# A 256-token two-layer block: 64 tokens of the product-key expert layer gathered row by row for VectorE, the other 192 with u in native fp32

## The chip, the cores and the metric

One Trainium2 chip, one of its NeuronCores. The metric is the device time of one execution in microseconds (us). The kernel is a single program written engine by engine: TensorE (PE), VectorE (DVE), ScalarE (ACT), GpSimd (POOL) and SyncE (SP, which only issues DMAs), with every wait written out by hand.

## What is computed

The reference is two transformer-like layers over 256 tokens of width 1024. The change concerns the expert layer (PEER) at the end of the first. Each token has 8 heads; each head picks 16 of 16384 experts by product keys; `u` and `v` are 16384 x 1024 fp32 tables.

```python
q = (h @ w_q).reshape(B, S, 8, 2, 128)
sc = einsum('bshpd,phnd->bshpn', q, keys)
v1, i1 = top_k(sc[..., 0, :], 16); v2, i2 = top_k(sc[..., 1, :], 16)
best, pos = top_k((v1[..., :, None] + v2[..., None, :]).reshape(..., 256), 16)
idx = take_along_axis((i1[..., :, None] * 128 + i2[..., None, :]).reshape(..., 256), pos)
gates = softmax(best)
act = gelu(einsum('tkd,td->tk', u[idx], h))        # 128 picks a token
out = einsum('tk,tkd->td', gates * act, v[idx])
```

## The kernel before

**How the work is staged.** All weights, about 240 MB, stream through the chip once, in 512 KB units of 128 partitions x 1024 fp32 (the table `STREAMS`): 18 + 4 + 16 + 4 + 4 + 8 units of the first layer's mixers, 16 of `w_pq`, then 128 units of `u`, 128 of `v`, then the second layer. SP fetches unit i into `raw[i % 4]` once unit i-4 has been used up.

**How a unit is multiplied.** TensorE's fp32r product keeps fewer bits than fp32, so every operand is split in two: ACT rounds the unit into `whi` (helper `act`, line 1154), DVE or POOL subtracts to get `wlo` (helper `tt`, line 1712, or POOL's line 2555), three slots each (`NSPL = 3`), and PE does three products (line 433):

```python
def three(o, a, b, start, stop):
    mm(o, a[0], b[0], start, False)
    mm(o, a[0], b[1], False, False)
    return mm(o, a[1], b[0], False, stop)
```

**The dense expert layer.** Rather than gather, the kernel computes all experts for all 256 tokens. Stage u (`lin_T`, 128 units): unit n holds 128 experts; 8 stationary tiles of 128 x 128 against `hTh`/`hTl` (normed tokens, transposed), 256 columns, 24 matmuls a unit; ACT applies the gelu to two units at a time from a PSUM bank into `acts`. Stage v (128 units): unit n's 128 experts are the contraction; `acts[:, n, :]` is split into two halves (`cut_acts`, one ACT and one DVE instruction of 256 columns) and is the stationary operand, `down(b, m, h)` for two token blocks b and two halves h of the width, 12 matmuls of 512 columns a unit, added up in banks 0 to 3 over all 128 units.

**Routing and gates.** What is not picked must be weighted with zero. `routing(b)` on DVE finds, for the tokens of block b, the picks and gates (MAX, MATCH_REPLACE, MAX_INDEX and compares); PE transposes them (line 442, three transposes a block); DVE copies them to `iT`, `row_b`, `col_b`, `gate2`. `gates(half)` builds, for 8 tokens at a time, one-hot matrices on DVE (`build`: `oh`, `og_eq`, `og`), multiplies them on PE (16 small matmuls) and multiplies `acts` by the result on DVE (`weigh`): 32 groups a half, 64 in all.

**What sets the order.** Side work is written as generators in a `Side` list; each engine calls `side.step()` once behind each unit, so that the same step of each engine's generator stands beside the same unit. `routing(0)`, `routing(1)` run in the first 62 units of u (`U1_STEPS` gives the number of steps behind each unit), then `side.drain()`; `gates(0)` in the last 66 units of u, `gates(1)` in the first 62 of v. POOL makes `wlo` for the first 62 units of u (`on_pool`), DVE for the others. DVE's loop over v runs two units ahead:

```python
for n in range(128):
    lo(BASE["v"] + n + 2)
    if n == 62:
        side.drain()
    cut_acts(n + 2)
    side.step()
```

SP's queue has the constants of the second layer (`con2`, 1345 KB) and `gf`, `w2c`, `mem` between units of v. `bridge()` adds the banks into `xres` behind stage v and normalises.

## Time and profile before

| | |
|---|---|
| median of 3 runs | 1445.1 us (1443.62 to 1445.19) |
| profiled execution, first to last instruction (span) | 1441.8 us |
| between the span and the median of the runs | 3.3 us |
| DMA moved | 245 MB |
| stage u, units 1 to 62, from the trace's clock | 266.0 to 444.8 us |
| stage u, units 63 to 128 | 444.8 to 654.3 us |
| stage v | 654.3 to 1034.0 us |

The page gives the profiled execution its span; no other time of its own is given for it, so the span stands for it. All times inside are on the span's clock. A busy PE means that some matmul was in flight; how fast they follow one another is read from start to start, since their durations overlap.

### The profile page before, as it was taken

The numbers are of one execution on the slowest core, as the hardware profiler recorded it, in microseconds if no ns is written. First come the engines' busy times: TensorE is split into PE (matmuls) and PEld (weight loads), VectorE is DVE, ScalarE is ACT, GpSimd is POOL, SyncE is SP. The second block draws the span as 40 slices with busy tenths as digits, with TensorE's granted clock in tenths as the row PEclk, the third lists the DMA queues.
The fourth block names the chain that finished last, engine by engine and source line by source line (L and its number), as shares of the span: only waits on it lengthen the run. The fifth ranks groups of instructions, "written<-read, shape, count | busy, mean of one in ns | idle before, by whom it ended". The sixth has DMA issues, their size and how long they took to land.

```text
span 1441.8 us, 25221 instructions
## 1 busy us (share of the span) xinstructions
PE 1422.6 (99%) x10281; PEld 1290.2 (89%) x10281; DVE 967.4 (67%) x1752; ACT 738.5 (51%) x1066; POOL 212.7 (15%) x122
## 2 busy tenths in 40 slices
PE   8999999999999999999999999999999999999997
PEld 7989989999999999998777778888899788899986
DVE  5565674693944777778888876655577864677754
ACT  5674654545454444444444445544567754655543
POOL 5000000488883000000000000000114100000000
PEclk9999999999999999999999999999999999999999
DMA  6433456455555545445545466555543453455552
GB/s 241 142 132 125 138 157 216 141 186 180 187 180 182 170 162 174 164 164 173 174 164 174 164 222 245 181 185 188 175 147 118 159 177 112 154 188 185 181 190 103
DMA packets 67219, 245.07 MB, mean 170 GB/s; under 512 B 7456, under 2 KB 7712, under 8 KB 66848
## 3 DMA queue, kind: packets, MB, share of 16 engines
q1 hardware_dynamic: 66960, 243.19, 50.5%
q8 instruction: 82, 1.34, 0.4%
q14 instruction: 33, 0.27, 0.1%
q10 hardware_dynamic: 144, 0.26, 0.0%
HBM read 242.37 MB, written 1.05 MB: 169 GB/s over the span
## 4 chain that ended last, share of the span: by engine, by line
PE 77%; issue 14%; DVE 4%; ACT 4%; POOL 1%; DMA 0%; POOLq 0%; SPq 0%; DVEq 0%; ACTq 0%
PE bank L433 76%; ACT A L1154 2%; DVE wlo L1712 1%; ACT whi L1154 1%; PE bank L442 1%; DVE A L1712 1%; ACT L1154 1%; DVE A L1708 0%; DVE xres L1712 0%; DMA xres<-in_x 0%; POOL wlo L2555 0%; ACT hTh L1154 0%; DVE small L2361 0%; DVE small L1712 0%; POOL small L2561 0%
## 5 line engine op out<-in xcount | busy, mean ns | idle before, releaser
L1712 DVE TENSOR_TENSOR wlo<-raw,whi 128x1024 fp32r<-128x1024 f32 (+1 forms) x375 | 458.1, 1223 | 334.3 <-ACT whi L1154 333.9
L1154 ACT ACTIVATE whi<-raw 128x1024 fp32r<-128x1024 f32 (+1 forms) x450 | 472.9, 1053 | 401.3 <-PE bank L433 401.3
L433 PE MATMUL bank<-hTh,whi 128*128 128x256 f32 x1944 | 555.5, 286 | 2.0 <-DVE wlo L1712 1.3
L433 PE MATMUL bank<-hTl,whi 128*128 128x256 f32 x1944 | 548.6, 282 | 0.0
L433 PE MATMUL bank<-hTh,wlo 128*128 128x256 f32 x1944 | 548.0, 282 | 0.0
L433 PEld LDWEIGHTS bank<-hTh,whi 128*128 128x128 f32 x1944 | 367.0, 189 | 5.9 <-DVE wlo L1712 2.1
L433 PEld LDWEIGHTS bank<-hTh,wlo 128*128 128x128 f32 x1944 | 366.0, 188 | 0.0
L433 PEld LDWEIGHTS bank<-hTl,whi 128*128 128x128 f32 x1944 | 365.5, 188 | 0.3 <-issue 0.2
L433 PE MATMUL bank<-whi,hTh 128*128 128x512 f32 (+2 forms) x552 | 218.4, 396 | 0.2
L433 PE MATMUL bank<-wlo,hTh 128*128 128x512 f32 (+2 forms) x552 | 215.0, 390 | 0.0
L433 PE MATMUL bank<-whi,hTl 128*128 128x512 f32 (+2 forms) x552 | 214.9, 389 | 0.0
L2555 POOL TENSOR_TENSOR wlo<-raw,whi 128x1024 fp32r<-128x1024 f32 x73 | 175.2, 2401 | 267.6 <-ACT whi L1154 263.7
L1154 ACT ACTIVATE A<-bank 128x512 f32<-128x512 f32 (+2 forms) x163 | 90.7, 563 | 225.9 <-PE bank L433 216.2
L2561 POOL TENSOR_TENSOR small<-small 128x1 f32<-128x1 f32 x16 | 9.5, 593 | 935.9 <-DVE small L1709 932.1
L433 PEld LDWEIGHTS bank<-whi,hTl 128*128 128x128 f32 x552 | 104.0, 188 | 23.8
L433 PEld LDWEIGHTS bank<-whi,hTh 128*128 128x128 f32 x552 | 104.1, 189 | 23.4 <-DVE wlo L1712 0.8
L433 PEld LDWEIGHTS bank<-wlo,hTh 128*128 128x128 f32 x552 | 104.2, 189 | 22.2
L433 PE MATMUL bank<-A 128*128 128x128 f32 (+9 forms) x472 | 69.9, 305 | 0.0
L433 PEld LDWEIGHTS bank<-A 128*128 128x128 f32 (+4 forms) x472 | 59.5, 183 | 6.5 <-issue 2.5
L1712 DVE TENSOR_TENSOR hTl<-A,hTh 128x256 fp32r<-128x256 f32 x126 | 52.6, 418 | 0.5 <-ACT hTh L1154 0.5
L1154 ACT ACTIVATE hTh<-A 128x256 fp32r<-128x256 f32 x126 | 50.6, 401 | 1.9 <-DVE A L1715 1.9
L1715 DVE SCALAR_TENSOR_TENSOR A<-bank,A 128x512 f32<-128x512 f32 (+1 forms) x76 | 49.4, 658 | 2.3 <-PE bank L433 2.2
(178 smaller groups left out, 1391.8 us busy)
## 6 DMA issues: line engine op xcount, KB each, us to landing
raw<-in_u SPq DMA_DIRECT2D x128, 512.0 KB, 3.3
raw<-in_v SPq DMA_DIRECT2D x128, 512.0 KB, 3.3
raw<-in_w_up SPq DMA_DIRECT2D x44, 512.0 KB, 3.3
raw<-in_w_down SPq DMA_DIRECT2D x22, 512.0 KB, 3.2
raw<-in_w_in_t SPq DMA_DIRECT2D x17, 512.0 KB, 3.4
raw<-in_w_in_g SPq DMA_DIRECT2D x16, 512.0 KB, 3.3
raw<-in_w_out SPq DMA_DIRECT2D x16, 512.0 KB, 4.0
raw<-in_w_pq SPq DMA_DIRECT2D x16, 512.0 KB, 3.5
```

The lines of the kernel that those rows point to most:

```text
L433: return e.matmul(o, l, r, start=st, stop=sp_, skip_group_check=True)
L442: return e.transpose(o, i, ident[0:k, 0:k])
L1154: return e.activation(o, i, func, **kw)
L1712: return e.tensor_tensor(o, a, b, op)
L1715: return e.scalar_tensor_tensor(o, a, z, b, op0, op1, **kw)
L2555: e.tensor_tensor(l, raw[i % NRAW][:, :], h.bitcast(F32), ALU.subtract).then_inc(s["lo_pool"], 1)
L2561: e.tensor_tensor(st[:, 2:3], st[:, 3:4], mhalf, ALU.pow).then_inc(s["n_rstd"], 1)
```

## The change

The tokens are divided: tokens 64 to 255 (`TD` = 192) stay in the dense computation; tokens 0 to 63 (`TG` = 64) leave it.

- **Stage u** (`lin_u`): PE multiplies `raw` itself by `h_full` (the tokens in fp32, one DVE add before the stage) in native fp32: 8 matmuls of 192 columns a unit. No `whi`, no `wlo` for u, on any engine; `raw[i % 4]` is free when PE is done with it.
- **Stage v**: `mixed_block` (4 matmuls a unit) has a stationary operand of which 64 columns are the low halves of tokens 64 to 127 and 64 the high halves; the two parts of its result are in the partitions 0 to 63 and 64 to 127 of banks 0 and 1 and are added at the end (`v_low`, `fold`). `dense_block` (6 matmuls) is the old product for tokens 128 to 255. 10 matmuls of 512 columns a unit. `cut_acts`: 192 columns, two ACT instructions and one DVE.
- **Gates**: 24 groups a half; `gates(1)` begins 16 steps later.
- **The 64 tokens**: 64 x 128 picks are 8192 rows of u and as many of v, 4 KB each. Two tokens' halves share the partitions (64 picks in partitions 0 to 63, the other 64 picks of the same tokens in 64 to 127), so one indirect DMA of POOL's fetches 128 rows, 512 KB, into one of 6 buffers `got`. 64 such gathers of `u_rows`, 64 of v, 67 MB in all. DVE takes each (`take`): for u one multiply with `h_rows` that also sums along the row (a dot product a partition), for v one multiply-add into `v_sum`. `due(n)` says how many takes are done by unit n: none before unit 26, then one every second unit, one a unit for units 62 to 127, and one every second unit of v until 86. ACT makes the gelu of 16 dots at a time at units 78, 94, 110 and 126 (`COEF_AT`). `fold_rows` sums the two halves on PE at unit 118 of v.
- **Moved**: `U1_STEPS` goes from 66 steps in 62 units to (1, 1, 1, 2); SP's four constant loads stand at other units of v; the second layer's memory norm 20 units later; `routing` storage and other tiles at other addresses.

```diff
+def is_u(i):
+    return BASE["u"] <= i < BASE["v"]
+def hi_count(i):
+    return i + 1 - min(max(i + 1 - BASE["u"], 0), 128)
...
-    if BASE["u"] <= slot < BASE["u"] + 62:
-        return True
...
+        if is_u(i):
+            out.append(("w", i + 1))
+            continue
...
-U1_STEPS = (1,) * 13 + (2,)
+U1_STEPS = (1, 1, 1, 2)
...
+def due(n):
+    if n < 26:
+        return 0
+    if n < 62:
+        return (n - 24) // 2
+    if n < 128:
+        return 19 + n - 62
+    return 85 + (n - 128) // 2
+COEF_AT = (78, 94, 110, 126)
...
+            def lin_u(n0, n1, steps=(1,)):
+                for n in range(n0, n1):
+                    i = BASE["u"] + n
+                    bk = 4 + pair[0] % 3
+                    if n % 2 == 0:
+                        use(bk)
+                    e.wait_ge(s_raw[i % NRAW], 16 * (i // NRAW + 1))
+                    wv = t3(raw[i % NRAW][:, :], KD)
+                    for k in range(KD):
+                        ins = mm(banks[bk][:, n % 2 * 256:n % 2 * 256 + TD], wv[:, k, :], hTf[:, k, TG:T], k == 0, k == KD - 1)
+                    ins.then_inc(s["w"], 1)
...
+                def mixed_block(m, h):
+                    w = wv[m - both[0]]
+                    for part in range(2):
+                        ins = mm(banks[h][:, :], cut(m, BOTH_M), w[part][:, h * 512:(h + 1) * 512], m == 0 and part == 0,
+                                 m == 127 and part == 1)
+                    return ins
+                def dense_block(m, h):
+                    w = wv[m - both[0]]
+                    return three(banks[2 + h][:, :], [cut(m, z) for z in (HI_D, LO_D)],
+                                 [z[:, h * 512:(h + 1) * 512] for z in w], m == 0, m == 127)
...
+                    e.wait_ge(s["fold_in"], 2)
+                    for h in range(2):
+                        ins = mm(banks[h][TG:P, :], ident[0:TG, 0:TG], v_low[0:TG, h * 512:(h + 1) * 512], False, True)
+                    ins.then_inc(s["fold"], 1)
...
+                if n == 118:
+                    e.wait_ge(s["x_done"], 2 * PICKS)
+                    e.wait_ge(s["eye"], 1)
+                    for h in range(2):
+                        use(6 + h)
+                        ins = mm(banks[6 + h][0:TG, :], fold_rows, v_sum[:, h * 512:(h + 1) * 512])
...
+                if b == 0:
+                    e.wait_ge(s["rt_dve"], 2)
+                    for q, dst in enumerate((tab, tab_up)):
+                        z = slice(q * PICKS, q * PICKS + PICKS)
+                        stt(dst[0:TG, 0:PICKS].bitcast(U32), sel_i[1][0:TG, z], float(P), sel_i[0][0:TG, z], ALU.mult, ALU.add)
+                        e.tensor_copy(dst[0:TG, PICKS:2 * PICKS], bex[0:TG, z]).then_inc(s["x_tab"], 1)
...
+            def take(x):
+                g = x % PICKS
+                z = got[x % NBUF]
+                e.wait_ge(s_got[x % NBUF], 16 * (x // NBUF + 1))
+                if x < PICKS:
+                    if x == 0:
+                        e.wait_ge(s_dup, 16)
+                    stt(z, z, 1.0, h_rows, ALU.mult, ALU.mult, accum_out=dots[:, g:g + 1]).then_inc(s["x_done"], 1)
+                    return
...
+                    e.wait_ge(s["x_done"], x)
+                    stt(v_sum, z, coef[:, g:g + 1], v_sum, ALU.mult, ALU.add).then_inc(s["x_done"], 1)
...
+            tt(hTf[:, :, TG:T], hTv[0][:, :, TG:T].bitcast(F32), hTv[1][:, :, TG:T].bitcast(F32), ALU.add).then_inc(s["h_full"], 1)
             side.lists[0] += [routing(0), routing(1)]
-            lin_T(BASE["u"], 62, steps=U1_STEPS)
+            lin_T(BASE["u"], 62, None, take_due, steps=U1_STEPS)
             side.drain()
             side.lists[0] += [gates(0), gates(1)]
-            lin_T(BASE["u"] + 62, 66)
+            lin_T(BASE["u"] + 62, 66, None, lambda u: take_due(u + 62))
...
+                take_due(n + 128)
                 side.step()
...
+            e.wait_ge(s["h_rows"], 1)
+            e.dma_start(h_rows[TG:P, :], h_rows[0:TG, :]).then_inc(s_dup, 16)
+            e.wait_ge(s["x_tab"], 2)
+            e.dma_start(tab[TG:P, :], tab_up[0:TG, :]).then_inc(s_tab, 16)
+            e.wait_ge(s_tab, 16)
+            e.wait_ge(s["sc_pe"], 8)
+            v_rows = wdram["v"].rearrange("n p d -> (n p) d")
+            for x in range(2 * PICKS):
+                g = x % PICKS
+                if x >= NBUF:
+                    e.wait_ge(s["x_done"], x - NBUF + 1)
+                e.indirect_dma_start(got[x % NBUF], None, u_rows if x < PICKS else v_rows,
+                                     bass.IndirectOffsetOnAxis(ap=tab[:, g:g + 1].bitcast(U32), axis=0)
+                                     ).then_inc(s_got[x % NBUF], 16)
+                if x == 2 * PICKS - 1:
+                    rstd(2)
```

**Where instructions stand now.** Three places carry the prediction. The first is PE's order at the second block's transposes in the first 62 units of u (`keep` holds the identity, `A` the picks). Before, they stand behind unit 56 of u:

```order
L433 MATMUL bank<-hTh,whi 128x256
L433 MATMUL bank<-hTl,whi 128x256
L433 MATMUL bank<-hTh,wlo 128x256
L442 MATMUL bank<-keep,A 128x128 [waits s_sc_act,s_rt_dve]
L442 MATMUL bank<-keep,A 128x128 x2
L433 MATMUL bank<-hTh,whi 128x256 [waits s_ev_act,s_lo_pool]
```

Of the change (behind unit 48 of u; the first block's stand behind unit 24):

```order
L494 MATMUL bank<-h_full,raw 128x192 [waits s_raw1]
L494 MATMUL bank<-h_full,raw 128x192 x7
L503 MATMUL bank<-keep,A 128x128 [waits s_sc_act,s_rt_dve]
L503 MATMUL bank<-keep,A 128x128 x2
L494 MATMUL bank<-h_full,raw 128x192 [waits s_raw2,s_ev_act]
```

A unit is 8 matmuls that wait for the DMA alone, and the same transposes with the same wait on DVE (`s_rt_dve`) come 8 units of u earlier.

The second is DVE's order where `routing(1)` nears the gates of block 1 (`picks` holds dots and coefficients, `G` the gathered rows). Of the change:

```order
L1828 TENSOR_TENSOR A<-bank,A 128x512 x3
L1831 SCALAR_TENSOR_TENSOR G,picks<-G 128x1024 [waits s_got2]
L2152 TENSOR_REDUCE A<-A 128x128 [waits s_own_dve]
L1828 TENSOR_TENSOR bank<-A,bank 128x512 [waits s_own_dve]
L1828 TENSOR_TENSOR bank<-A,bank 128x512 x3
L1828 TENSOR_TENSOR A<-bank,A 128x512 [waits s_own_dve]
L1828 TENSOR_TENSOR A<-bank,A 128x512 x3
L1831 SCALAR_TENSOR_TENSOR G,picks<-G 128x1024 [waits s_got3]
L2152 TENSOR_REDUCE A<-A 128x128 [waits s_own_dve]
L2155 TENSOR_REDUCE A<-A 128x8 [waits s_rt_act]
L2157 RECIPROCAL A<-A 128x8 [waits s_own_dve]
L1828 TENSOR_TENSOR A<-A 128x128 [waits s_own_dve]
```

The takes are new rows inside the routing; ten of them stand between the first block's `iT` copy and the last row shown, whose end the second transposes wait for.

The third is DVE's order in the first 47 units of v. Of the change, two units:

```order
L1828 TENSOR_TENSOR wlo<-raw,whi 128x1024 [waits s_hi]
L1828 TENSOR_TENSOR hT<-A,hT 128x192 [waits s_ca_hi]
L1828 TENSOR_TENSOR wlo<-raw,whi 128x1024 [waits s_hi]
L1828 TENSOR_TENSOR hT<-A,hT 128x192 [waits s_ca_hi]
L1831 SCALAR_TENSOR_TENSOR G<-G,picks 128x1024 [waits s_x_done,s_got2]
L1831 SCALAR_TENSOR_TENSOR A<-bank,A 128x64x8 [waits s_g_pe,s_ev_act]
L1828 TENSOR_TENSOR oh<-iota_b,row_b 128x1024 [waits s_g_pe]
L1828 TENSOR_TENSOR og_eq<-iota_b,col_b 128x512 [waits s_g_og]
L1828 TENSOR_TENSOR og<-og_eq,gate 128x1024 [waits s_own_dve]
```

Before, the same eight rows without the take, and with 256 in place of 192.

## Rows read from the trace of the kernel before

**Rows 1.** The page, part 1: busy us of each engine (share of the span), instructions

```profile
PE 1422.6 (99%) x10281; PEld 1290.2 (89%) x10281; DVE 967.4 (67%) x1752; ACT 738.5 (51%) x1066; POOL 212.7 (15%) x122
```

**Rows 2.** Stretches (first us:last us length, busy per engine (instructions), PEclk, DMA share, GB/s)

```profile
266.00:444.80 178.80, 178.80 (x1493) 178.80 (x1493) 119.36 (x452) 87.63 (x100) 147.52 (x62) 1.00 0.54 178
...
654.30:1034.00 379.70, 379.59 (x2048) 303.19 (x2049) 270.50 (x397) 178.91 (x271) 1.10 (x2) 1.00 0.56 188
```

**Rows 3.** Timeline of PE (start us, length us): fp32r products of 512 columns, two gate groups

```profile
701.32 0.40 PE L433 MATMUL bank<-whi,hTh 128*128 128x512 f32 x1
701.55 0.40 PE L433 MATMUL bank<-wlo,hTh 128*128 128x512 f32 x1
...
451.01 0.66 PE L433 MATMUL bank<-og,oh 128*128 128x64 f16 x16
...
647.27 0.66 PE L433 MATMUL bank<-og,oh 128*128 128x64 f16 x16
```

**Rows 4.** Timeline of PE: runs of fp32 products of 128 and of 256 columns

```profile
258.89 7.31 PE L433 MATMUL bank<-A 128*128 128x128 f32 x64
...
1202.88 3.62 PE L433 MATMUL bank<-A 128*128 128x256 f32 x16
```

**Rows 5.** Groups by shape, whole span: durations of those products and of a load (mean ns)

```profile
L433 PE MATMUL bank<-A 128*128 128x256 f32 x80 | 18.6, 378 | 0.0
L433 PE MATMUL bank<-A 128*128 128x128 f32 x136 | 16.2, 275 | 0.0
...
L433 PEld LDWEIGHTS bank<-A 128*128 128x128 f32 x312 | 42.3, 191 | 3.4 <-issue 1.2 <-DVE A L1712 0.2
```

**Rows 6.** Timeline of DVE in the routing (in brackets the idle time before, and who ended it)

```profile
347.21 0.56 DVE L2048 COPY iT<-bank 128x384 f32<-128x384 f32 x1 [19.19 <-PE bank L442]
...
408.56 0.41 DVE L1712 TENSOR_TENSOR A<-A 128x128 f32<-128x128 f32 x1
428.17 0.56 DVE L2048 COPY iT<-bank 128x384 f32<-128x384 f32 x1 [19.20 <-PE bank L442]
```

**Rows 7.** The nearest rows to a take: a product of this shape, and a sum read

```profile
L1715 DVE SCALAR_TENSOR_TENSOR A<-A 128x1024 f32<-128x1024 f32 x1 | 1.3, 1277 | 0.0
...
209.19 0.08 DVE L1715 DVE_READ_ACCUMULATOR A<-xres 128x1 f32 x1
209.31 0.22 DVE L1709 TENSOR_SCALAR small<-small 128x1 f32<-128x1 f32 x1
```

**Rows 8.** Timeline of DVE at the first gate groups (stage u, with wlo on DVE)

```profile
447.03 1.23 DVE L1712 TENSOR_TENSOR wlo<-raw,whi 128x1024 fp32r<-128x1024 f32 x1 [15.03 <-ACT whi L1154]
448.17 0.68 DVE L1712 TENSOR_TENSOR oh<-iota_b,row_b 128x1024 f16<-128x1024 f16 x1
...
449.83 1.22 DVE L1712 TENSOR_TENSOR wlo<-raw,whi 128x1024 fp32r<-128x1024 f32 x1
```

**Rows 9.** Groups of DVE by shape, 660 to 840 us (busy us, mean ns, idle before)

```profile
L1712 DVE TENSOR_TENSOR wlo<-raw,whi 128x1024 fp32r<-128x1024 f32 x59 | 72.0, 1221 | 26.1 <-ACT whi L1154 26.1
L1712 DVE TENSOR_TENSOR hTl<-A,hTh 128x256 fp32r<-128x256 f32 x59 | 24.6, 418 | 0.0
L1715 DVE SCALAR_TENSOR_TENSOR A<-bank,A 128x512 f32<-128x512 f32 x29 | 19.8, 682 | 0.0
```

**Rows 10.** A 20 us stretch of stage v with gates, and the densest DMA of the trace

```profile
700.00:720.00 20.00, 20.00 (x128) 15.88 (x127) 17.17 (x28) 8.74 (x13) 0.00 (x0) 1.00 0.51 165
...
8.00:16.00 8.00, 6.95 (x57) 6.38 (x55) 7.09 (x22) 6.18 (x15) 7.09 (x7) 1.00 0.99 377
```

**Rows 11.** DMA issues: KB each, median us from issue to landing

```profile
raw<-in_u SPq DMA_DIRECT2D x128, 512.0 KB, 3.3
A<-in_gf SPq DMA_DIRECT2D x2, 512.0 KB, 4.6
```

**Rows 12.** Timeline: DVE beside a POOL instruction of two SBUF inputs

```profile
1045.40 2.79 POOL L2623 TENSOR_TENSOR A<-A 128x128 f32<-128x128 f32 x4
1045.93 1.47 DVE L1712 TENSOR_TENSOR wlo<-raw,whi 128x1024 fp32r<-128x1024 f32 x1
```

More of the change, by code:

```diff
@@ L33 @@
 GATE_UP = 2.0 ** 15
+TG = 64
+TD = T - TG
+NG = TD // OB
+NBUF = 6
+PICKS = 64
 STREAMS = [
@@ L156 @@
 own_act own_dve own_pool zeros x_sq hi_half lo_half lo_first f_xg f_xd f_act hd_mask
+h_full h_rows x_tab x_done x_act x_sum x_pe fold_in fold eye
 """.split()
+def due(n):
[7 more added lines that the diff above has]
+COEF_AT = (78, 94, 110, 126)
 class Own:
@@ L194, in until, with build @@
             self.step()
-def build(nc, x, mem, wdram, keep_d, con0_d, con1_d, con2_d, keys_d, w2c_d, gf_d, gf2_d, out):
+def build(nc, x, mem, wdram, keep_d, con0_d, con1_d, con2_d, keys_d, w2c_d, gf_d, gf2_d, gx_d, u_rows, out):
     ctx = ExitStack()
@@ L211, in build @@
         xres = sb("xres", 2048)
-        hTh = sb("hTh", 2048, F32R)
-        hTl = sb("hTl", 2048, F32R)
+        with ExitStack() as c:
+            sb("hT_first", 2048, c=c)
+            h_full = sb("h_full", 2048, c=c)
+        hT = sb("hT", 4096, F32R)
+        hTh, hTl = hT[:, 0:2048], hT[:, 2048:4096]
         small = sb("small", 256)
@@ L584, in lin_T @@
                     side.step(steps[(i + 1) % len(steps)])
+            def lin_u(n0, n1, steps=(1,)):
[9 more added lines that the diff above has]
+                    ins.then_inc(s["w"], 1)
+                    if n % 2:
+                        by, n_ev = PAIR_FREED[pair[0]]
+                        free[bk] = (s[by], n_ev)
+                        pair[0] += 1
+                    side.step(steps[(i + 1) % len(steps)])
             def lin_A(u0, src, K, N, bks, ready, pair=True, split=None):
@@ L777, in gates @@
                 o2 = og[:, :].rearrange("p (m j i r) -> p m j i r", m=OP, j=2, r=2)
-                for g in range(T // OB):
-                    G = 32 * half + g
+                for _ in range(16 * half):
+                    yield
+                for g in range(NG):
+                    G = NG * half + g
                     bk = gate_bank(half, g)
@@ L2063, in gates @@
                 lo64 = 64 * half
+                for _ in range(16 * half):
+                    yield
                 e.wait_ge(s["rt_dve"], 8)
@@ L2099, in gates, with take_due @@
                     yield
-                weigh(T // OB - 1)
+                weigh(NG - 1)
+            taken = [0]
+            def take(x):
[7 more added lines that the diff above has]
+                    return
+                if g % 16 == 0:
+                    c = slice(g, g + 16)
+                    e.wait_ge(s["x_act"], g // 16 + 1)
+                    own(tt(coef[:, c], coef[:, c], tab[:, PICKS + g:PICKS + g + 16], ALU.mult))
+                    again()
+                if g == 0:
+                    ts(v_sum, z, coef[:, 0:1], None, ALU.mult).then_inc(s["x_done"], 1)
+                else:
+                    e.wait_ge(s["x_done"], x)
+                    stt(v_sum, z, coef[:, g:g + 1], v_sum, ALU.mult, ALU.add).then_inc(s["x_done"], 1)
+            def take_due(n):
+                while taken[0] < min(due(n), 2 * PICKS):
+                    take(taken[0])
+                    taken[0] += 1
             def cut_acts(n):
@@ L2122, in bridge @@
             def bridge():
-                add_and_sum("v", 0, BASE["v"] + 128, 3)
+                e.wait_ge(s["fold"], 1)
+                for h in range(2):
+                    z = xres[TG:P, h * 512:h * 512 + 512]
+                    tt(z, banks[h][TG:P, :], z, ALU.add).then_inc(s["r_add"], 1)
+                add("v", 0, BASE["v"] + 128, 1, 0)
+                rms_sum(3, 0)
+                add("v", 0, BASE["v"] + 128, 1, 1)
                 yield
```

188 lines of the change are left out of this document (119 added, 69 removed).

## The prediction

> **What bounds the kernel now.** I read the page first: PE is busy 99% of the span, DVE 67% [rows 1]. Then stretches of the two stages that change: PE is never idle and its clock is granted at 1.00 (2.4 GHz), DMA has nearly half its time free, DVE is busy 119 of 179 us in the first 62 units of u and 271 of 380 in v [rows 2]. So PE sets the pace from 266 to 1034 us, and what counts is how fast matmuls follow one another. That is read from the timeline, start to start: 0.234 us for fp32r on 512 columns [rows 3]. Last I read DVE's rows, since the change adds work there while PE gets faster.
>
> **PE, stage u.** A unit takes 178.8 / 62 = 2.88 us [rows 2]. The new unit is 8 native fp32 products of 192 columns. The trace has such products at 128 and 256 columns; the 32 scores of this program show as 64 records, so one product is two. 64 records take 7.31 us with a last one of 0.275: (7.31 - 0.275) / 63 = 0.112 us apart. At 256 columns (3.62 - 0.378) / 15 = 0.216 [rows 4, 5]. 192 lies halfway: 0.164, two records 0.328, a unit 2.62 us. Saved: 128 x 0.26 = **-33**.
>
> **PE, gates.** Two units and a group take (647.27 - 451.01) / 31 = 6.33 us [rows 3], less 2 x 2.88 leaves 0.57. 16 groups fewer: **-9**.
>
> **PE, stage v.** 379.7 us less 32 groups (18.1) and some 2 us of other transposes is 2.81 a unit, 12 x 0.234 [rows 2, 3]. Now 10 x 0.234 = 2.34. Saved: 128 x 0.47 = **-60**. PE alone would give -102.
>
> **DVE in the first 62 units of u: a new stall.** Before, the transposes of the two blocks stood 28 and 56 units into u, and DVE waited 19.2 us for each, until 347.21 and 428.17 [rows 6]. They now stand behind units 24 and 48, with shorter units. First block: 266 + 24 x 2.62 = 328.9; DVE was ready at 347.2 - 19.2 = 328.0. Just in time. Second block: DVE needs 347.21 to 408.97 = 61.8 us [rows 6], and now ten takes. The nearest rows are a product of this shape (1.28 long; neighbours start 0.08 before the end, so 1.20 apart) and the 0.12 that reading a sum adds [rows 7]: 1.32 each, 75 us in all. PE is there after 24 x 2.62 + 0.5 = 63.4. It waits **+12**. Behind the waiting transposes is the rest of u; nothing else can run on PE. The gather itself is not late: the index table is complete before the first block's transposes, the first take some 9 us behind them, and two small DMAs and a gather of 3.3 us [rows 11] fit. A PE that stood still for 12 us may fall to the lower clock level (1.2 for 2.4 GHz), which no row of these stages shows; between 0 and one and a half units at double length (4 us) I take **+1.5**.
>
> **Units 63 to 128 of u.** DVE loses wlo (1.14) and gets a take (1.32), with half a group of gates (2.26 / 2, [rows 8, 9]): 2.45 of PE's 2.90. Covered. DMA is not so safe: 1.05 MB a unit, in (66 x 2.62 + 24 x 0.57) / 66 = 2.83 us, is 370 GB/s; the densest rows moved 377 at 99% of the engines' time [rows 10], the usual rate 178 at 54%, or 330 [rows 2]. I take the former, as the two queues overlap: the 18 units without gates want 400 and lengthen by 0.16 each, **+3**; the other end is 66 x (1.05 / 0.330 - 2.83) = +23. The Trainium skill, DMA: Bandwidth & Descriptors, § Where 436 GB/s comes from, has about 358 GB/s for a core's HBM reads as the binding limit; by it this stretch lasts 69.2 MB / 358 = 193 us and the term is +7. The trace exceeds that figure, if only for 8 us.
>
> **First 47 units of v: DVE becomes the bound.** For two units and a group DVE does: two wlo at 1.14 (448.17 - 447.03), build 1.66 (449.83 - 448.17) [rows 8], weigh 0.60, two cuts of now 192 columns at 0.27 (0.34 before) [rows 9], a take without a sum read 1.20: 6.28 us. PE does 2 x 2.34 + 0.57 = 5.25. Without the take and with the wide cuts my count gives 2.61 a unit, and the trace 17.17 / 20 of 3.10 = 2.66 [rows 10], so it is not too high. 23.5 x 1.03 = 24, less the 2 us by which DVE is ahead at the start: **+22**. Who waits is PE, at the gate matmuls and at wlo. From unit 47 to 86 DVE has 1.14 + 0.27 + 0.60 = 2.01 of 2.34: covered.
>
> **GpSimd beside DVE.** A wlo beside a POOL instruction took 1.47 for 1.22 us [rows 12]. Where DVE binds there are some 33 gathers; at 0 to 0.25 each that is 0 to 8, I take **+3**.
>
> **Constants in v.** con2, gf, w2c and mem (3.6 MB) now share units 60 to 88 with gathers: 28 x 0.79 + 3.6 = 25.6 MB in 66 us is 390 GB/s. At 377 **+2**, at 330 +12.
>
> **The end of v.** The sum of the halves and the fold are eight records of up to 0.43 us on PE, an ACT copy between them of which some 0.5 us shows, and two more adds of 0.6 on DVE before the norm, which is on the path: **+3** (2 to 6).
>
> Nothing for: ACT (it loses its roundings of u, and in v one small instruction more a unit, at most 0.3 us, makes 179 + 38 of some 320 us, [rows 2]), the DVE add for `h_full` (some 1.7 us, beside 7.3 us of scores, [rows 4]), SP (as many units, freed earlier), POOL's lost wlo (147.5 us, [rows 2]), which never bound.
>
> **Sum**: -102 + 12 + 1.5 + 22 + 3 + 3 + 2 + 3 = -56 (rounded). The profiled span is 1441.8 us, so 1386; the median of the runs shown stands 3.3 higher: **1389**.
>
> **Rivals.**
> - *DMA binds.* The random 4 KB rows move no faster than the usual 330 GB/s. Then +23 for +3 and +12 for +2, or 1419. For it: no row shows 370 GB/s for more than 8 us, and u's ring gives a fetch only three units' time. Against: rows of 4 KB are what the streams have too.
> - *The port is locked.* Each gather holds DVE while its descriptors are written. With POOL's shortest run in the rows (2.79 / 4 = 0.7 us) on the 33 takes that count: +23, less the 3: 1409. For: the slowed wlo [rows 12]; against: it lost 0.25 us and not the whole of POOL's 0.7. The Trainium skill, SBUF — State Buffer, § SBUF: two separate sides, says the shared pair of ports is an exclusive lock for a whole instruction, taken also by a VectorE op with two SBUF inputs against a GpSimd op that reads SBUF. By its words, wlo and takes are such, and this time is the result; the row shows a smaller share.
> - *Native fp32 is held by its weight loads.* If 192 columns cannot go faster than a load lasts, 0.191 us a record [rows 5] instead of 0.164, a unit takes 3.06 us: +56, less the 12 of the stall: 1433. Against: at 128 columns records follow at 0.112 [rows 4], below a load's length, as loads overlap. This is the way in which the change would not do what it says.
> - *Slower than before: the gathers come too slowly.* One gather a unit is needed in units 63 to 128 of u, DVE takes them in order, and the gates stand behind them on DVE, PE behind the gates. If one gather follows another by G us, this stretch costs 66 x (G - 2.83): the whole gain is gone at G = 2.83 + 56 / 66 = 3.7 us. A transfer of 512 KB with another pattern took 4.6 to land [rows 11]; if gathers are that slow and don't overlap, the time is 1389 + 117 = 1506. Against: six buffers let five be in flight, and 3.3 us to land [rows 11] is latency, not pitch.
>
> **Chances.** Forecast 0.63; DMA binds 0.17; port lock 0.08; weight loads 0.03; slow gathers 0.09. Within 0.2% (2.9 us, about what a measurement can tell from no change) lies only a narrow part of the last two: 0.02. Faster 0.90, slower 0.08. The low end takes the small terms at zero and DVE's excess at 18: -102 + 12 + 18 + 2 = -70, 1375, and 7 below it for the read of the pitches; the high end reaches past the DMA rival to 1424. Range 1368 to 1424.
>
> **What the profile would show.** Right: u units 2.62 us apart with record starts at 0.16; v units at 2.34 behind the gates; PE idle once for 10 to 14 us before the second block's transposes, ended by DVE; DVE at 95% or more in the first 47 units of v and PE waiting for it there some 22 us; DMA at 90% or more in units 63 to 128 of u. Wrong: waits of DVE for a DMA into `G` (slow gathers), PE waiting for a DMA into `raw` in u (DMA binds), wlo and takes longer than 1.5 us (port), or records 0.19 apart (weight loads). A u stage without the stall would mean that I misread the steps.

## The result, and the profile after

The changed kernel takes **1384.57 us** (median of 4 runs, 1382.58 to 1386.59) against 1445.14 us before (4 runs, 1443.62 to 1445.28): a ratio of 0.9585, 95% interval 0.9571 to 0.9598. The forecast was 1389 in a range of 1368 to 1424. The profiled span fell from 1441.8 to 1384.8 us, by 57.0. That the total fits so well is luck: it hides two terms of some ten microseconds each that were wrong in opposite directions, and most of what follows is about them.

First the page, part 1, of the changed kernel (it answers to [rows 1]), then stretches of it (first us:last us length, busy time and instructions of PE, PEld, DVE, ACT and POOL, PEclk, DMA share, GB/s; they answer to [rows 2, 10]).

```profile
PE 1334.3 (96%) x8752; PEld 1203.9 (87%) x8753; DVE 989.8 (71%) x1828; ACT 620.3 (45%) x1136; POOL 221.3 (16%) x190
```

```profile
396.00:440.60 44.60, 43.76 (x259) 43.49 (x260) 15.96 (x31) 3.87 (x14) 14.40 (x11) 0.96 0.88 314
...
458.00:600.00 142.00, 142.00 (x1137) 140.34 (x1135) 109.09 (x172) 14.12 (x53) 67.40 (x54) 1.00 1.00 369
600.00:625.00 25.00, 21.07 (x129) 20.77 (x128) 6.52 (x9) 6.89 (x20) 3.75 (x4) 1.00 0.96 371
625.00:780.00 155.00, 133.72 (x872) 103.11 (x873) 151.87 (x220) 69.98 (x144) 24.64 (x26) 0.98 0.79 251
```

Read them one by one. In 396 to 440 us (units 49 to 64 of u) VectorE is idle for two thirds of the time: room that the schedule of takes does not use. From 458 to 600 the DMA share reads 1.00 and PE is not held up at all (another run below moves more at the same share, so that 1.00 does not mean that nothing more goes through). In 600 to 625, the end of u, PE loses 4 us although VectorE has almost nothing to do. From 625 to 780 (the gates' part of v) VectorE is busy 98% and PE only 86%: VectorE is the bound there, as forecast.

Behind v nothing changed: the first matmul of the next stage starts at 977.10 us instead of 1034.23, which is 57.1 earlier, the whole of the gain.

The places where PE stands still show in its timeline (start us, length us, and in brackets the idle time before and what ended it; answers to [rows 3, 6]):

```profile
329.44 0.49 PE L503 MATMUL bank<-keep,A 128*128 128x128 f32 x3
329.77 63.40 PE L494 MATMUL bank<-h_full,raw 128*128 128x192 f32 x384
395.96 0.55 PE L503 MATMUL bank<-keep,A 128*128 128x128 f32 x3 [2.79 <-DVE A L1828]
...
446.47 0.64 PE L494 MATMUL bank<-og,oh 128*128 128x64 f16 x16
...
452.23 0.64 PE L494 MATMUL bank<-og,oh 128*128 128x64 f16 x16
...
625.51 0.80 PE L494 MATMUL bank<-og,oh 128*128 128x64 f16 x16 [3.88 <-DVE og L1828]
628.19 0.76 PE L494 MATMUL bank<-whi,first 128*128 128x512 f32 x1 [1.88 <-DVE first L1828]
628.76 0.63 PE L494 MATMUL bank<-wlo,first 128*128 128x512 f32 x1
...
654.34 0.48 PE L494 MATMUL bank<-whi,hT 128*128 128x512 f32 x1
...
660.11 0.66 PE L494 MATMUL bank<-og,oh 128*128 128x64 f16 x16 [0.84 <-DVE og L1828]
...
822.62 0.47 PE L494 MATMUL bank<-whi,hT 128*128 128x512 f32 x1 [1.98 <-DVE hT L1828]
```

The rows give the unit of u, (452.23 - 446.47 - 0.55) / 2 = 2.60 us (0.55 is the group of gates); the stall before the second block's transposes, 2.8 us and not 12; a stop of 3.9 and 1.9 us at the start of v, which the forecast does not have; and a stop of 2.0 us at 822, where constants are loaded (PE waits there for `hT` of VectorE, VectorE for ScalarE, and ScalarE 4.6 us for a DMA into `raw`).

### The profile page after: what moved, and what is told of

Same layout as the page of the kernel before. It is cut to its first block, busy times and chain, and to the rows that moved or that the text cites. A ratio compares the mean times of both kernels' runs of the same rounds, so it can differ in the third digit from the quotient of the medians.

```text
span 1384.8 us, 22298 instructions
## 1 busy us (share of the span) xinstructions
PE 1334.3 (96%) x8752; PEld 1203.9 (87%) x8753; DVE 989.8 (71%) x1828; ACT 620.3 (45%) x1136; POOL 221.3 (16%) x190
## 3 DMA queue, kind: packets, MB, share of 16 engines
HBM read 309.75 MB, written 1.05 MB: 224 GB/s over the span
## 4 chain that ended last, share of the span: by engine, by line
PE 57%; DVE 19%; issue 15%; ACT 5%; DMA 3%; POOL 1%; POOLq 0%; DVEq 0%; SPq 0%; ACTq 0%
PE bank L494 56%; DVE wlo L1828 5%; DVE G L1831 3%; ACT A L1255 2%; ACT whi L1255 2%; DVE A L1828 1%; DMA raw<-in_v 1%; DMA raw<-in_u 1%; DVE og L1828 1%; DVE hT L1828 1%; PE bank L503 1%; DVE oh L1828 1%; DVE A L1831 1%; ACT L1255 1%; DVE A L1824 1%
## 5 line engine op out<-in xcount | busy, mean ns | idle before, releaser
L1255 ACT ACTIVATE whi<-raw 128x1024 fp32r<-128x1024 f32 (+1 forms) x322 | 337.7, 1052 | 261.9 <-PE bank L494 232.8
L494 PE MATMUL bank<-h_full,raw 128*128 128x192 f32 x2048 | 341.9, 328 | 1.7 <-DMA raw<-in_u 1.4
L494 PE MATMUL bank<-hT,whi 128*128 128x256 f32 x1840 | 338.3, 284 | 2.0 <-DVE wlo L1828 1.3
L494 PEld LDWEIGHTS bank<-h_full,raw 128*128 128x128 f32 x2048 | 333.6, 191 | 3.0 <-issue 1.2
L494 PE MATMUL bank<-whi,hT 128*128 128x512 f32 (+2 forms) x852 | 290.4, 393 | 2.8 <-DVE hT L1828 2.6
L494 PEld LDWEIGHTS bank<-hT,whi 128*128 128x128 f32 x1840 | 284.3, 189 | 6.2 <-DVE wlo L1828 2.1
L494 PE MATMUL bank<-hT,wlo 128*128 128x256 f32 x920 | 259.7, 282 | 0.0
L494 PE MATMUL bank<-wlo,hT 128*128 128x512 f32 (+2 forms) x552 | 215.6, 391 | 0.0
L494 PEld LDWEIGHTS bank<-whi,hT 128*128 128x128 f32 x852 | 159.0, 189 | 42.2 <-DVE wlo L1828 5.1
L494 PEld LDWEIGHTS bank<-hT,wlo 128*128 128x128 f32 x920 | 172.6, 188 | 0.0
L1831 DVE SCALAR_TENSOR_TENSOR G<-G,picks 128x1024 f32<-128x1024 f32 x63 | 80.6, 1279 | 10.1 <-DMA G<-in_v,picks 9.4
```

The lines of the kernel that those rows point to most:

```text
L494: return e.matmul(o, l, r, start=st, stop=sp_, skip_group_check=True)
L1255: return e.activation(o, i, func, **kw)
L1831: return e.scalar_tensor_tensor(o, a, z, b, op0, op1, **kw)
```

## The experiments

Two theories at the start. **A**: the time is what the forecast's steps say, corrected by the rows above: VectorE's sum binds the first 47 units of v (+22), a stall of 2.8 us at the second transposes, and a start of v that costs 8 us (5.8 idle, the rest at the low clock level: from 628.19 to 632.87 the fp32r products are 0.43 us apart instead of 0.234). **B**: not VectorE's work but the traffic of 67 MB of gathered rows holds the kernel, and the takes only look guilty because they stand where the waits are.

### Takes moved out of the part where VectorE binds, and into it: `late`, `early`

```diff
-    return 85 + (n - 128) // 2
+    if n < 174:
+        return 85
+    return 85 + (n - 174) * 5 // 8
```

(`late`; GpSimd's `rstd(2)`, which the norm of `mem` waits for, is put behind gather 118 instead of the last, since gathers now go on behind that norm.) Expected:

> The 43 takes of v that stand in the change at one per two units from v unit 0 are moved to units 47 to 115 (five per eight units); the gathers follow. Theory A (VectorE's sum binds the first 47 units of v): two units and a group need 6.28 - 1.20 = 5.08 us of VectorE, less than PE's 5.25, so groups of gates stand 5.25 apart instead of 6.27 and 22 of them give back 23 us; at the start of v two takes fewer stand ahead of the first matmul (-2); later units have 1.14 + 0.27 + 0.63 x 1.2 = 2.16 of PE's 2.34, covered, and the gathers meet the constants (0 to +3). 1384.6 - 23 - 2 + 2 = 1361 (1357 to 1367). Theory B (PE waits there for the chain build - matmul - weigh and not for VectorE's sum): groups stay 6.27 apart, 1380 to 1385. Theory C (the work is only moved, and VectorE binds later instead): half or less of the gain, 1372 or more, with PE waiting for wlo behind unit 47.

```diff
-    return 85 + (n - 128) // 2
+    return 85 + n - 128
```

> The same takes at one per unit in the first 43 units of v. Theory A: two units and a group need 6.28 + 1.20 = 7.48 us of VectorE, groups 7.5 apart until unit 43, 21 takes more in the bound part, +25; the load of constants at units 60 to 88 meets no gathers any more (-2 to -4): 1407 (1402 to 1412). Theory B: no more than +5, since the sum does not bind.

Measured: `late` 1368.69 us (1367.51 to 1376.35, 5 runs), ratio to before 0.9502 (0.9476 to 0.9527); `early` 1406.15 us (1405.15 to 1408.0), ratio 0.9737 (0.9724 to 0.9751). The groups of gates of `late`, then those of `early`, in PE's timeline:

```profile
700.94 0.66 PE L496 MATMUL bank<-og,oh 128*128 128x64 f16 x16
706.20 0.66 PE L496 MATMUL bank<-og,oh 128*128 128x64 f16 x16
```

```profile
709.03 0.66 PE L494 MATMUL bank<-og,oh 128*128 128x64 f16 x16 [2.05 <-DVE og L1828]
716.53 0.66 PE L494 MATMUL bank<-og,oh 128*128 128x64 f16 x16 [2.08 <-DVE og L1828]
```

5.26 us apart without takes, 6.27 with one per two units, 7.5 with two: the second take costs its own length, the first that less the 0.2 us that VectorE had to spare, and without takes PE's 5.25 is what is left. Theory A holds to 0.1 us per group. But `late` gave 16 us of the 23: it missed the expected 1361 by 8 (and two of its five runs took 1376). Its takes meet other things behind unit 47. PE is idle there for some 6.5 us (2.7 in 780 to 800, 1.7 before 853.76, 2.1 before 887.77), each time until `hT` of VectorE, while ScalarE waits for a DMA into `raw` 22 times in 740 to 960 us. The stretches of `late`:

```profile
780.00:800.00 20.00, 17.26 (x74) 13.64 (x73) 15.08 (x20) 9.78 (x21) 6.78 (x5) 1.00 0.99 378
...
840.00:860.00 20.00, 18.27 (x77) 14.13 (x77) 16.86 (x20) 10.99 (x23) 7.29 (x6) 1.00 1.01 386
```

The start of v did not get the 2 us either (3.86 and 1.66 idle): the takes in front of it come due at units 126 and 127 of u and at v's first, as before.

### VectorE's work and the traffic taken out one after the other: `thin`, `none`

```diff
-                    stt(z, z, 1.0, h_rows, ALU.mult, ALU.mult, accum_out=dots[:, g:g + 1]).then_inc(s["x_done"], 1)
+                    tt(dots[:, g:g + 1], z[:, 0:1], h_rows[:, 0:1], ALU.mult).then_inc(s["x_done"], 1)
...
-                    stt(v_sum, z, coef[:, g:g + 1], v_sum, ALU.mult, ALU.add).then_inc(s["x_done"], 1)
+                    stt(v_sum[:, 0:8], z[:, 0:8], coef[:, g:g + 1], v_sum[:, 0:8], ALU.mult, ALU.add).then_inc(s["x_done"], 1)
```

> All gathers stay, at the same places, but a take touches 1 column (u) or 8 columns (v) instead of 1024, which leaves out the 64 tokens' products. This prices VectorE's part of the takes alone. Theory A: the stall before the second block's transposes goes (-3 to -4 with its low clock), the first 47 units of v go at PE's pace (-23), the start of v loses two takes (-2): 1355 (1351 to 1359). A rival, that the gathers' traffic and not the takes holds the kernel: less than -15, 1370 or more.

`none` is `thin` without `e.indirect_dma_start(...)` in GpSimd's loop; the small takes read `h_rows` in place of the gathered rows and wait for no gather.

> As before with takes of 1 and 8 columns, and without the 128 gathers: the 64 tokens' rows are not fetched. The difference to the run with gathers prices the DMA traffic and GpSimd. Theory A: -1.4 for the two waits for raw in u, -3 at the start of v (the first unit of v lands sooner behind the last ones of u), -3 at the load of constants: 1355 - 7 = 1348 (1344 to 1352), and what remains over 1343 (PE alone) is the start of v, where whi and wlo must be made before the first matmul. Rival (contention: instructions or matmuls get shorter too): 1340 or less. Rival (traffic costs nothing): 1353 or more.

Measured: `thin` 1354.62 us (1351.89 to 1356.72), ratio 0.938 (0.9367 to 0.9392); `none` 1346.36 us (1344.99 to 1347.9), ratio 0.9324 (0.9311 to 0.9337). Both came within 2 us. So of the 38 us that the 64 tokens' path costs, the takes on VectorE are 30 and the gathers 8. Theory B falls: traffic alone is the small part. And 1346 without either is 3 above the 1343 that PE's terms of the forecast (-102) give alone.

The start of v tells the two apart. ScalarE and PE there in `thin` (traffic, hardly any work), then in `none`:

```profile
612.32 1.06 ACT L1255 ACTIVATE whi<-raw 128x1024 fp32r<-128x1024 f32 x1 [2.42 <-DMA raw<-in_v]
...
616.49 0.66 PE L494 MATMUL bank<-og,oh 128*128 128x64 f16 x16 [1.98 <-DVE og L1828]
618.12 0.76 PE L494 MATMUL bank<-whi,first 128*128 128x512 f32 x1 [0.97 <-DVE first L1828]
```

```profile
608.90 1.06 ACT L1255 ACTIVATE whi<-raw 128x1024 fp32r<-128x1024 f32 x1 [0.58 <-DMA raw<-in_v]
...
614.71 0.47 PE L494 MATMUL bank<-whi,first 128*128 128x512 f32 x1 [0.97 <-DVE first L1828]
```

u ends at another time in each run, so I count from there. The first product of v starts 6.9 us behind the last of u in the change, 3.9 in `thin`, 2.1 in `none`; ScalarE gets the first unit 6.6, 5.8 and 4.0 us after PE is done with the tile that it lands in. So the start of v has both causes: some 3 us are takes and some 2 are traffic. In the change and in `thin`, products at the low level of the clock come on top.

### The second stall: `steps`

```diff
-U1_STEPS = (1, 1, 1, 2)
+U1_STEPS = (1, 1, 1, 1, 1, 1, 2)
```

> The transposes of the two blocks stand behind 27 and 53 units of u instead of 24 and 48: between them PE has 26 x 2.605 + 0.4 = 68.1 us of work, VectorE 65.9 (as in the change, 329.97 to 395.9). If the 2.8 us of idle PE and the low clock behind it (0.93 of 20 us, 1.4) are the whole price of the stall: no idle PE at the second transposes, clock 1.00, 1384.6 - 4.2 = 1380.4. A rival, that the work comes due elsewhere (the first group of gates waits for VectorE at unit 62): no gain, 1384 or more. With my forecast's 12 + 1.5 the gain would have been 13.5.

Measured: 1380.61 us (1377.2 to 1382.76), ratio 0.9557 (0.9543 to 0.9571), 4.0 us less than the change. The second transposes of `steps` stand without idle time:

```profile
394.80 10.56 PE L494 MATMUL bank<-h_full,raw 128*128 128x192 f32 x64
405.20 0.49 PE L503 MATMUL bank<-keep,A 128*128 128x128 f32 x3
```

The whole stall is worth 4, where the forecast had 13.5.

### Why it was so short: `pool_busy`

Before, VectorE needed 61.8 us for a block [rows 6], and I added ten takes to that. Those 61.8 us of the kernel before hold rows that are much longer than their like in the change. First VectorE before (the first two) and GpSimd before, then VectorE in the change:

```profile
348.33 0.23 DVE L2057 CAST gate<-iT 128x128 f16<-128x128 f32 x1
348.59 2.45 DVE L1712 TENSOR_TENSOR gate<-iT,gate 128x128 f16<-128x128 f32 x1
...
389.29 2.41 DVE L2020 CAST A<-A 128x256 f32<-128x256 uint32 x1
...
348.50 2.39 POOL L2555 TENSOR_TENSOR wlo<-raw,whi 128x1024 fp32r<-128x1024 f32 x1 [0.91 <-ACT whi L1154]
```

```profile
331.36 0.29 DVE L1828 TENSOR_TENSOR gate<-iT,gate 128x128 f16<-128x128 f32 x1
...
378.02 0.29 DVE L2136 CAST A<-A 128x256 f32<-128x256 uint32 x1
```

The suspicion: GpSimd's `wlo`, which the change removes, held them. So it was given such work again; the only other edit is that VectorE waits for the last of it before unit 62 of u:

```diff
+            e.wait_ge(s["own_pool"], 19)
...
                                      ).then_inc(s_got[x % NBUF], 16)
+                if x < 18:
+                    e.wait_ge(own.sem, own.n)
+                    own(e.tensor_tensor(W(0)[1], h_rows, h_rows, ALU.subtract))
```

> GpSimd does one tensor_tensor of 128 x 1024 with operands in SBUF, as its wlo of before, behind each of the first 18 gathers (its result is not used). Theory P (a GpSimd instruction on SBUF data holds the VectorE instructions that read two SBUF tiles or run in a fast mode; a gather does not): takes between the two transposes grow from 1.21 to up to 3.6 us where they meet one, some casts to 2.4, and the second stall grows by 3 to 10 us: 1388 to 1396. The rival, that before's casts of 2.4 us had another cause: takes 1.21, stall 2.8, 1384.6.

Measured: 1392.65 us (1390.87 to 1394.8, 4 runs), ratio 0.9641 (0.9627 to 0.9656), 8.1 us more than the change. Rows of VectorE and GpSimd of this run, and its second transposes:

```profile
331.66 2.48 DVE L1828 TENSOR_TENSOR gate<-iT,gate 128x128 f16<-128x128 f32 x1
...
344.83 3.17 DVE L1831 SCALAR_TENSOR_TENSOR G<-G 128x1024 f32<-128x1024 f32 x1
...
345.01 1.90 POOL L2801 TENSOR_TENSOR wlo<-G 128x1024 fp32r<-128x1024 f32 x1
...
402.70 0.90 PE L503 MATMUL bank<-keep,A 128*128 128x128 f32 x3 [10.07 <-DVE A L1828]
```

The same product that took 0.29 takes 2.48 again, a take grows by the whole 1.9 us of the GpSimd row, and the stall is 10.1 us. GpSimd's gathers do nothing of the kind: in the change, the 64 takes of u are 1.204 to 1.225 us long, and 30 of them stand beside a gather. There it is the gather that grows, from 0.94 us to 1.68 and more. GpSimd and VectorE in the change:

```profile
445.25 1.68 POOL L2795 DMA_INDIRECT G<-in_u_rows,picks  x1 [29.00 <-DVE G L1831]
447.23 0.94 POOL L2795 DMA_INDIRECT G<-in_u_rows,picks  x1 [0.30 <-issue]
...
444.90 1.22 DVE L1831 SCALAR_TENSOR_TENSOR G<-G 128x1024 f32<-128x1024 f32 x1
```

### Takes in front of the first wait of v: `start`

```diff
-        return 19 + n - 62
+        return min(19 + n - 62 + max(0, n - 122), 85)
```

> Three takes that stand in the change behind VectorE's wait for whi of v's first unit (at u units 126, 127 and v unit 0) are made due three units earlier, ahead of that wait, where VectorE stands still for 15.8 us. If VectorE's queue ends the wait of PE at the start of v (3.9 us before the gates, 1.9 before the first v matmul), two takes fewer stand ahead of that matmul: PE idle 5.8 - 2.4 = 3.4 us there, 1382. The rival: the raw tile of v's first unit lands late (620.28, 6.6 us behind the matmul that frees it) because gathers share the DMA; then nothing or less than 1 us is won, since the earlier gathers compete with it: 1384 or 1385.

Measured: 1386.18 us (1385.55 to 1388.22), ratio 0.9595 (0.9582 to 0.9608): not faster; the 1.6 more than the change is no larger than the scatter of its runs. The rival was right. PE's idle time at the start of v is 4.45 and 0.46 instead of 3.88 and 1.88, but ScalarE gets the first unit only at 623.20, 8.4 us after its tile is free instead of 6.6, since the next gathers were issued earlier too and went ahead of it (their last at 613.22 instead of 605.89). What the shorter queue gave, the later landing took.

### The gathers kept away from the first fetch of v: `free_start`

```diff
-U1_STEPS = (1, 1, 1, 2)
+U1_STEPS = (1, 1, 1, 1, 1, 1, 2)
...
-    if n < 62:
+    if n < 52:
         return (n - 24) // 2
     if n < 128:
-        return 19 + n - 62
+        return min(14 + n - 52, 85)
```

> With the transposes behind 27 and 53 units of u (1380.6), takes come due faster from unit 52 of u, where VectorE is idle, and stop at 85 from unit 123, so that no take stands behind the wait for whi of v's first unit and the six gathers ahead of them are done some 15 us before that unit's raw tile is fetched. If the start of v is held by that tile's late landing (gathers beside it) and by two queued takes: the tile lands in some 3 us instead of 6.6, PE's idle 5.8 us shrinks to 1 to 2 and the 4.7 us at the low clock behind it go too (-2): 1375 (1373 to 1377). If the landing has nothing to do with the gathers: only the two takes, 1379.

Measured: 1373.07 us (1371.74 to 1376.34), ratio 0.9515 (0.9502 to 0.9528), 7.5 less than `steps` (6 by the two ratios to before). ScalarE in the change, then ScalarE and PE in `free_start`:

```profile
620.28 1.06 ACT L1255 ACTIVATE whi<-raw 128x1024 fp32r<-128x1024 f32 x1 [3.26 <-DMA raw<-in_v]
```

```profile
612.42 1.06 ACT L1255 ACTIVATE whi<-raw 128x1024 fp32r<-128x1024 f32 x1 [0.63 <-DMA raw<-in_v]
...
616.46 0.66 PE L494 MATMUL bank<-og,oh 128*128 128x64 f16 x16
617.95 0.47 PE L494 MATMUL bank<-whi,first 128*128 128x512 f32 x1 [0.84 <-DVE first L1828]
```

ScalarE gets the unit 4.0 us after its tile is free, as in `none`, and no take stands in VectorE's queue. PE now passes into v with 0.84 us of idle time, and the first product of v is 0.47 long and not 0.76: the clock did not fall (granted 1.00 from 610 to 630 us). This edit takes away the late landing and the queued takes at once, and does not say which was worth more.

### What DMA can move: `k6_thin`

`thin`, with 6 of the 8 products of a unit of u (`for k in range(6)`), which leaves out the last quarter of the sum over the model dimension.

> The run with gathers and takes of 1 and 8 columns, and u with 6 of its 8 products a unit (the last quarter of the sum over the model dimension is left out): PE needs 1.95 us a unit, with gates 4.46 for two units, DMA wants 2.1 MB for them. This shows what DMA can move. If about 400 GB/s (the 20 us from 580 to 620 in the change): groups of gates 5.25 apart. If 358 to 370 GB/s (as in 460 to 560, where PE was busy throughout): 5.7 to 5.9, as with 8 products. In the first 48 units VectorE's routing (55 us a block without takes) binds: PE stalls 8 to 9 us at both transposes. In all 1354.6 - 24 - 15 = 1316 for 400 GB/s, 1330 for 360.

Measured: 1322.73 us (1321.39 to 1322.89, 4 runs), ratio 0.9158 (0.9144 to 0.9172). The stretch of u with gathers and gates, and PE's timeline within it:

```profile
440.00:580.00 140.00, 127.85 (x958) 115.78 (x957) 49.40 (x126) 15.22 (x57) 49.16 (x52) 1.00 1.03 409
```

```profile
488.28 0.65 PE L494 MATMUL bank<-og,oh 128*128 128x64 f16 x16
...
491.35 2.22 PE L494 MATMUL bank<-h_full,raw 128*128 128x192 f32 x12 [0.28 <-DMA raw<-in_u]
493.40 0.65 PE L494 MATMUL bank<-og,oh 128*128 128x64 f16 x16
```

With PE wanting more, the two queues moved 409 GB/s for 140 us, and groups of gates stand 5.12 us apart. That is above the 330 and the 377 that the forecast weighed, and the DMA share reads 1.03, hardly more than the 1.00 at 369 GB/s in the change. The change wants 1.05 MB a unit, 364 GB/s with gates and 402 without: below it, if only just. The time itself came out between the two that I had given: PE also waits for `raw` from 332 to 354 us (4.3 in nine waits) and again behind the second transposes (4.1 in 387 to 412), which I had not counted.

### Three products of 192 columns: `three_products`

```diff
+                        if n < 62:
+                            ins = three(o, [t3(z, KD)[:, k, :] for z in W(0)], [z[:, 96 * k:96 * k + TD] for z in W(1)], k == 0, k == KD - 1)
```

> The first 62 units of u use 24 fp32r matmuls of 192 columns a unit instead of 8 native fp32 products (on tiles of other units: the logits of these experts are wrong, the time is that of the form, without the rounding on ScalarE and VectorE that it would need). If an fp32r matmul's time goes with its columns (0.120 at 256, 0.234 at 512): 0.090 apart, 2.17 a unit against 2.605, so native fp32 costs PE 0.43 a unit more than three products of the same columns would, and all of u's gain on PE comes from the 64 columns left out; DVE's routing then binds and PE stalls some 9 us more at both transposes, so that the whole time falls by only some 27 - 18 = 9: 1376. If fp32r below 256 columns is slower, as fp32: 0.16 or more, 3.9 a unit, 1384.6 + 80.

Measured: 1390.46 us (1388.38 to 1392.52, 4 runs), ratio 0.9637 (0.9622 to 0.9652). Three fp32r products of 192 columns of this run:

```profile
266.77 0.28 PE L494 MATMUL bank<-whi 128*128 128x192 f32 x1
266.88 0.27 PE L494 MATMUL bank<-wlo,whi 128*128 128x192 f32 x1
266.99 0.27 PE L494 MATMUL bank<-whi,wlo 128*128 128x192 f32 x1
```

They are 0.111 apart, not 0.090: a unit takes 24 x 0.111 = 2.67 us, a little more than native fp32's 2.60. Both of my cases were wrong. At 256 columns three products are cheaper than native fp32 (3 x 0.120 = 0.36 against 2 x 0.216 = 0.43 [rows 4]), at 192 they are no longer.

### The loads of constants, and all together: `late_const`, `tuned`

```diff
-            fetch_to(BASE["v"] + 66)
...
+            fetch_to(BASE["v"] + 104)
+            e.dma_start(A3[:, NCON2:NCON2 + D], gf_d.partition_broadcast(P)).then_inc(s_gf, 16)
+            fetch_to(BASE["v"] + 120)
+            e.dma_start(A3[:, 0:NCON2], con2_d).then_inc(s_con2, 16)
+            fetch_to(BASE["v"] + 125)
+            e.dma_start(A3[:, NCON2 + D:NCON2 + D + 1536], w2c_d).then_inc(s_w2c, 16)
```

> The run with late takes (1368.7), its loads of con2, gf and w2c moved from v units 66 to 80 to units 104 to 125; mem stays at 88. In the late run DMA was busy 95 to 101% from 760 to 860 us and PE stood still 2.7 us in 780 to 800 and 1.7 in 840 to 860, and VectorE 2.1 at the norm of mem. If the bursts of constants on top of gathers cause the first two: they go, 1368.7 - 5 = 1364. If the gathers alone fill DMA there: 1368 as before.

`tuned` has the edits of `free_start`, these loads, `rstd(2)` behind gather 122, and for v:

```diff
-    return 85 + (n - 128) // 2
+    if n < 174:
+        return 85 + (n - 128) // 14
+    if n < 224:
+        return 88 + (n - 174) * 16 // 25
+    return 120 + max(0, n - 232) * 2 // 3
```

> All together: transposes behind 27 and 53 units, takes of u faster from unit 52, none due across the start of v, three in the first 46 units of v (the slack of 0.17 us per two units), 40 in units 47 to 115 with a pause at the norm of mem, constants later. 1384.6 - 4 (second stall) - 6 (start of v) - 23 (VectorE in the first 47 units) + 1 to 4 (DMA in units 47 to 115) = 1353 (1350 to 1357). If the gains overlap or DMA takes them back: 1360 or more.

Measured: `late_const` 1364.01 us (1362.86 to 1366.7), ratio 0.9449 (0.9436 to 0.9462), as expected; `tuned` **1357.54 us** (1354.93 to 1359.54), ratio 0.9403 (0.939 to 0.9416). It beats both kernels, by 27 us against the change, but is 4.5 short of what was summed. Where the rest stays, in PE's timeline and in a stretch of `tuned`:

```profile
844.97 0.77 PE L498 MATMUL bank<-whi,hT 128*128 128x512 f32 x1 [4.73 <-DVE hT L1832]
```

```profile
840.00:860.00 20.00, 15.27 (x60) 12.11 (x59) 16.30 (x21) 11.62 (x25) 6.71 (x4) 0.91 0.89 320
```

One wait of 4.7 us, at the load of `mem` (1 MB at unit 88) on top of two takes in three units, where ScalarE waits 6.6 us for a DMA into `raw`; in `late_const` the same place costs PE 2.3. A slower rate of takes just there was not tried.

## Why the prediction was right in sum, and where it was not

| term | forecast | measured |
|---|---|---|
| PE, unit of u | -33 (2.62) | -36 (2.60) |
| PE, 16 groups of gates | -9 | -9 |
| PE, v | -60 | -60 |
| stall before the second transposes, with clock | +12 + 1.5 | +2.8 + 1.4 |
| DMA in units 63 to 128 of u | +3 | +1.4 |
| first 47 units of v, VectorE | +24 | +22 |
| start of v | -2 | +8 |
| GpSimd beside VectorE | +3 | 0 |
| constants | +2 | +4 |
| start of u | 0 | +1 |
| end of v, and all that is not assigned | +3 | +7 |
| sum | -56 | -57 |

How the measured ones are worked out: unit and groups from the timeline above; clock terms are 20 us times what the granted clock of the stretch lacks (0.93 in 380 to 400: 1.4; 0.91 in 820 to 840: 1.8, beside 2.0 idle); the DMA term is the two waits for `raw` in u (0.84, which stands in the 59th unit, and 0.57); (6.27 - 5.25) x 22 groups is 22; the start of v is 5.8 idle and 4.7 us spent on 2.6 us of products; u starts at 267.04 instead of 265.96. The last row is what the others leave of the 57.

**PE's terms** came out within 3 us. Halfway between 128 and 256 columns was a good read of 192, and the units of v are 10 x 0.234 to the digit.

**The first 47 units of v**: right in mechanism and size. VectorE's 6.28 for two units and a group was measured as 6.27, `late` and `early` moved it by one take each way, `thin` removed it.

**The second stall was the step that failed by most**: "Second block: DVE needs 347.21 to 408.97 = 61.8 us, and now ten takes ... 1.32 each, 75 us in all." It was 65.9. The 61.8 was a duration taken from a stretch in which another engine was at work that the change removes. Four of its rows were held by GpSimd's `wlo`, together 5.0 us longer than in the change (2.16 + 2.12 + 0.63 + 0.12), and 1.5 us of it was a wait for ScalarE, which had u's roundings in its queue. What is left is 55.3; a take costs 1.14 there and not 1.32, since the sum's read overlaps (a take starts at 336.88, the next instruction at 338.02), so 66.7. The forecast counts POOL's lost `wlo` as "never bound": true for GpSimd, but it bound VectorE.

**The rival of the locked port** read too little out of one row. "A wlo beside a POOL instruction took 1.47 for 1.22" [rows 12] is a short overlap: the GpSimd row merges four instructions of 0.46, 0.50, 1.43 and 0.50 us, and `wlo` lost only the rest of the second, while the third, which began beside it at 1046.29, grew to 1.43. `pool_busy` shows 3.17 for 1.21 and 2.48 for 0.29, the whole of a GpSimd instruction. The Trainium skill, SBUF — State Buffer, § SBUF: two separate sides, says that the loser of the shared ports fully blocks; for GpSimd's tensor_tensor these rows agree. For gathers, which I put under the same rule, takes of 1.22 us show no such hold on VectorE, so the term of 3 and the rival's 23 were both 0.

**The start of v was missed.** The forecast has there "less the 2 us by which DVE is ahead at the start". In u the matmuls read `raw` itself, so its tile is free only when PE is done with it, and the first unit of v must still be fetched, rounded and subtracted before its first matmul. PE left that tile at about 613.6 (five of the eight units that start at 600.59), the fetch beside gathers took until 620.28, 6.6 us, and two takes, a build and two `wlo` stood in VectorE's queue behind it. Of the passage from u to v, 6.9 us long, `thin` takes 3.0 away by the takes alone and `none` 1.8 more by the gathers. `start` shows that a shorter queue is worth nothing when the gathers that follow delay the landing, and `free_start`, which ends both, brought 7.5 us back.

**DMA does not bind**, as forecast. The Trainium skill, DMA: Bandwidth & Descriptors, § Where 436 GB/s comes from, puts the limit for a core's HBM transfers at about 358 GB/s; the change ran at 369 for 142 us without holding PE, and `k6_thin` moved 409. The measurement decides: +1.4 was right, not +7. Where DMA did cost something (8 us, `thin` against `none`), 1.6 us of it are there by the end of u; the rest came from bursts in front of a tile that was needed at once, at the start of v (1.8 us, and some 1.6 at the lower level of the clock) and at the constants (two waits of PE, 0.4 and 1.2).

The other rivals: weight loads did not hold native fp32 (0.163 apart), and waits of VectorE for a gather sum to 9.4 us in eight places (and 1.6 in each of two more), all where PE did not wait for VectorE. A stop at the first fetch of v stood in no rival.

The end of v with all that is not assigned is 7 where 3 was forecast. No run takes the sums at its end away, but the trace of the change prices them: each of the two holds PE for 1.86 us, and PE is idle for 0.5 at 970.28. The last of them, the fold, and the product behind it:

```profile
973.73 1.93 PE L494 MATMUL bank<-A,keep 64*64 64x512 f32 x4
975.59 0.51 PE L494 MATMUL bank<-whi,hT 128*128 128x512 f32 x1
```

That is some 4 us. Another 1.4 belongs to the second stall: from start to start it costs 3.8 us and not 2.8, and the ten units behind it 1.8 and not 1.4. What stays open is the rest, under 2 us, and the 1.0 us by which u starts later.

## What to carry to other kernels

A duration read from the trace belongs to what ran beside it: when a change takes work off one engine, look whether rows of another were longer than their like, and count those too. When matmuls begin to read the DMA's own buffers, look at the first unit of the next stage that needs a rounded copy: its fetch can start only when PE is done with the tile; keep other transfers out of the time before that first fetch. And when a table paces side work, give each part of the program its own rate: here 27 us lay in the places of the same 128 takes, of the transposes and of three loads of constants.
